# Ranking in two halves, earlier row stores, later x stores, and longer rings for the expert weights

## The chip, the cores and the metric

The program runs on one core of a Trainium2 chip, in fp32. The metric is the device time of one execution in microseconds (us). TensorE (PE), VectorE (DVE), ScalarE (ACT), GpSimd (POOL) and SyncE (SP) each work through their own instruction list in order, and wait for one another by semaphores. SP, ACT and POOL also issue DMA transfers.

## The reference, cut to what matters

There are two layers on 640 tokens: 512 latent ones (`NL`) and 128 context ones (`NC`), of width 1024. Each layer normalizes, modulates (factors computed from the conditioning by `w_mod`), runs two mixers, and then an expert-choice mixture of experts, where each of 16 experts picks its own tokens. This is done for the latent and for the context tokens apart:

```python
def ec_moe(x, w_router, w_gate, w_up, w_down):
    cap = EC_CAPACITY * t // N_EXPERTS          # 64 latent, 16 context
    aff = jax.nn.softmax(logits, axis=1)        # over the tokens
    gate, idx = lax.top_k(aff, cap)
    xs = jax.vmap(lambda xb, ib: xb[ib])(x, idx)
    hid = jax.nn.silu(xs @ w_gate) * (xs @ w_up)      # einsums, 1024 -> 512
    y = (hid @ w_down) * gate[..., None]              # 512 -> 1024
    return jax.vmap(lambda yb, ib: jnp.zeros((t, d), yb.dtype).at[ib].add(yb))(y, idx)
```

## The kernel before

An expert (`e` = 0 to 15) has 80 rows, 64 latent and 16 of the context. Its weights are six pieces of 1 MB (128 partitions x 2048 fp32): `g0`, `g1`, `u0`, `u1` (gate and up) and `d0`, `d1` (down). All weights of the kernel, the expert pieces among them, go through one list, `stream`, which SP works off in order: a piece is loaded into one of four slots of `stage` (`SLOTS`), piece p into slot p modulo 4, after the piece four places ahead of it has been used up. An expert piece m (0 to 95 in a layer, in the order gate and up of e + 1, then down of e) is used up when ACT has written its rounded copy (`w_hi`) and DVE the rest (`w_lo`, semaphore `lo_ready`). PE multiplies three times (hi by hi, hi by lo, lo by hi). Because a load waits on SP, every load behind it waits too.

Before the experts, the start of the MoE (semaphore names in brackets) goes like this:

- DVE ranks the affinities: eight rounds of MAX8, FIND_INDEX8 and MATCH_REPLACE8 over 512 columns, one row for each expert (L2130 to L2138); the context's rows are in the first two rounds. PE turns the lists (`gates`), and DVE writes `slots`, the row numbers.
- PE turns the five row tiles of h (`h`, 128 rows each), ACT evacuates each to one of four row buffers (`htok`) and stores it to `h_dram` (512 KB). The fifth waits until the first store has landed (`h_out`).
- In layer 1, PE also turns the five tiles of x (`x out`), and ACT stores them to `acc_dram` (`x_stored`), to which the experts' results are added.
- ACT writes the context's `slots` (`gates ctx`), behind all those stores in its order.
- POOL gathers the rows of the first four experts from `h_dram` (L780), when `slots` are written and the stores have landed; PE turns them, and the first expert's matmuls start.
- SP's load of piece 4 (L672) waits, besides for its slot, until gather(0) has landed.

For each expert, POOL also scatters: it adds 80 rows to `acc_dram` (L789). A scatter waits for the one before.

The lines of the load of an expert piece, and of the wait for a row buffer:

```python
                        if m == SLOTS:
                            sp.wait_ge(gathered[0], 16 * (E // AHEAD * L + 1))
                        sp.wait_ge(lo_ready, m + (moe_q[L] - SLOTS + 1))
...
                    if t == 4:
                        act.wait_ge(h_out[0], 16 * (2 * L + 1))
```

## Time and profile before

| | us |
|---|---|
| three runs: median (lowest to highest) | 1483.58 (1479.49 to 1487.28) |
| the profiled execution: time | 1485.16 |
| its span, first to last instruction | 1483.4 |
| busy in it: PE | 1275.2 (86%) |
| busy: DVE | 886.8 (60%) |
| busy: ACT | 736.8 (50%) |
| busy: POOL | 218.8 (15%) |

The busy shares are means over the whole execution, and its stages have different limits: each stage is read by itself. A DMA share is the mean busy share of the core's 16 DMA engines. A transfer's time runs from its issue until its data has landed.

### The profile page before, as it was taken

To read this page: it belongs to the slowest core of one execution; us is meant where nothing else is said; L and a number is where in the kernel's file an instruction comes from. 1 tells how busy PE (TensorE), PEld (TensorE's weight loads), DVE (VectorE), ACT (ScalarE), POOL (GpSimd) and SP (SyncE) were. 2 spreads that over 40 slices of the span, in tenths; PEclk is the share of its full clock that TensorE was granted. 3 is DMA by queue.
4 is the path that set the end of the run, shared out by engine and by line. 5 is a ranking of instruction groups with operands and counts; after the bars stand their busy time and mean duration, and the time that the engine had idled before them with its cause. 6 is when DMAs were issued, how large, how long until landed. Compare 5 with 4: busy or idle time off the path is not lost.

```text
span 1483.4 us, 18079 instructions
## 1 busy us (share of the span) xinstructions
PE 1275.2 (86%) x7500; PEld 919.3 (62%) x7500; DVE 886.8 (60%) x997; ACT 736.8 (50%) x866; POOL 218.8 (15%) x128
## 2 busy tenths in 40 slices
PE   5799988997499899999559999999976998999991
PEld 3796856893365555655149994667934655656550
DVE  3613456326688777787164452553257888888883
ACT  3531056415377676776144214453155666666662
POOL 3000000020112121211150000000202023333130
PEclk9897899999699999999779999799997999999996
DMA  9710180004899999999873222002049999999985
GB/s 346 223 61 29 58 298 31 1 29 174 280 324 361 352 355 358 351 366 355 294 211 97 76 61 98 1 1 86 29 170 315 333 351 347 354 347 354 359 311 169
DMA packets 99047, 323.19 MB, mean 218 GB/s; under 512 B 6367, under 2 KB 30142, under 8 KB 82582
## 3 DMA queue, kind: packets, MB, share of 16 engines
q1 hardware_dynamic: 87360, 283.54, 53.3%
q0 software_dynamic: 9152, 30.53, 8.0%
q10 hardware_dynamic: 2454, 7.96, 1.3%
q8 instruction: 60, 0.98, 0.3%
q14 instruction: 21, 0.17, 0.0%
HBM read 298.20 MB, written 23.81 MB: 217 GB/s over the span
## 4 chain that ended last, share of the span: by engine, by line
PE 48%; DMA 21%; ACT 13%; DVE 13%; issue 3%; POOL 1%; ACTq 0%; SPq 0%; POOLq 0%; DVEq 0%
PE psum L821 45%; DVE w_lo L1774 8%; DMA stage<-in_moe_w_up 6%; DMA stage<-in_moe_w_gate 5%; ACT w_hi L1676 5%; DMA stage<-in_moe_w_down 4%; ACT arena L1601 3%; DMA stage<-in_w_mod 2%; DVE arena L2050 2%; DMA h_dram<-arena 1%; DMA acc_dram<-arena 1%; ACT arena L1374 1%; POOL arena L706 1%; DVE h_lo L1774 1%; ACT arena L1423 1%
## 5 line engine op out<-in xcount | busy, mean ns | idle before, releaser
L1774 DVE TENSOR_TENSOR w_lo<-stage,w_hi 128x2048 fp32r<-128x2048 f32 (+1 forms) x216 | 490.7, 2280 | 192.7 <-ACT w_hi L1676 120.7
L1676 ACT ACTIVATE w_hi<-stage 128x2048 fp32r<-128x2048 f32 x192 | 366.6, 1913 | 153.4 <-DMA stage<-in_moe_w_gate 43.0
L821 PE MATMUL psum<-w_hi,h_hi 128*80 128x512 f32 (+1 forms) x848 | 332.4, 392 | 51.8 <-DVE w_lo L1774 40.8
L821 PE MATMUL psum<-w_lo,h_hi 128*80 128x512 f32 (+1 forms) x848 | 326.8, 385 | 0.0
L821 PE MATMUL psum<-w_hi,h_lo 128*80 128x512 f32 (+1 forms) x848 | 326.8, 385 | 0.0
L821 PE MATMUL psum<-h_hi,w_hi 128*128 128x320 f32 x672 | 211.8, 315 | 10.2 <-DVE h_lo L1822 10.2
L821 PEld LDWEIGHTS psum<-w_hi,h_hi 128*80 128x80 f32 (+1 forms) x848 | 130.2, 154 | 132.5 <-DVE w_lo L1774 40.7
L821 PE MATMUL psum<-h_lo,w_hi 128*128 128x320 f32 x672 | 210.3, 313 | 0.0
L821 PE MATMUL psum<-h_hi,w_lo 128*128 128x320 f32 x672 | 210.1, 313 | 0.0
L821 PEld LDWEIGHTS psum<-w_hi,h_lo 128*80 128x80 f32 (+1 forms) x848 | 130.1, 153 | 64.4 <-issue 2.5
L789 POOL DMA_INDIRECT acc_dram<-arena x32 | 94.3, 2946 | 478.7 <-ACT arena L1707 255.0
L821 PEld LDWEIGHTS psum<-w_lo,h_hi 128*80 128x80 f32 (+1 forms) x848 | 130.6, 154 | 53.9 <-issue 2.1
L821 PE MATMUL psum<-arena 128*64 128x128 f32 (+9 forms) x940 | 135.2, 394 | 15.4 <-ACT arena L1601 9.0
L821 PEld LDWEIGHTS psum<-h_hi,w_hi 128*128 128x128 f32 x672 | 128.7, 192 | 12.0 <-issue 12.0
L821 PEld LDWEIGHTS psum<-h_lo,w_hi 128*128 128x128 f32 x672 | 128.7, 191 | 0.2 <-issue 0.2
L821 PEld LDWEIGHTS psum<-h_hi,w_lo 128*128 128x128 f32 x672 | 128.6, 191 | 0.0
L1374 ACT ACTIVATE arena<-psum 128x256 f32<-128x256 f32 (+8 forms) x133 | 75.2, 616 | 103.9 <-PE psum L821 81.6
L821 PEld LDWEIGHTS psum<-arena 128*64 128x64 f32 (+4 forms) x940 | 79.4, 177 | 74.2 <-issue 51.4
L1601 ACT ACTIVATE arena<-psum,arena 128x640 f32<-128x640 f32 x64 | 50.3, 790 | 64.1 <-DVE arena L2050 64.1
L706 POOL TENSOR_TENSOR arena<-arena 128x640 f32<-128x640 f32 x24 | 39.0, 1626 | 282.3 <-ACT arena L1397 280.8
L1387 ACT ACTIVATE w_hi<-stage 128x2048 fp32r<-128x2048 f32 x22 | 42.0, 1913 | 73.6 <-PE psum L821 70.2
L2108 DVE SCALAR_TENSOR_TENSOR xT<-psum,mod,xT 128x320 f32<-128x320 f32 (+2 forms) x48 | 18.2, 434 | 88.1 <-PE psum L821 88.1
(224 smaller groups left out, 1198.5 us busy)
## 6 DMA issues: line engine op xcount, KB each, us to landing
stage<-in_moe_w_gate SPq DMA_DIRECT2D x64, 1024.0 KB, 8.4
stage<-in_moe_w_up SPq DMA_DIRECT2D x64, 1024.0 KB, 8.9
stage<-in_moe_w_down SPq DMA_DIRECT2D x64, 1024.0 KB, 7.3
stage<-in_w_mod SPq DMA_DIRECT2D x48, 1024.0 KB, 7.1
stage<-in_ev_w_in SPq DMA_DIRECT2D x7, 1024.0 KB, 11.8
stage<-in_od_w_in SPq DMA_DIRECT2D x7, 1024.0 KB, 9.9
h_dram<-arena ACTq DMA_DIRECT2D x10, 512.0 KB, 6.7
stage<-in_ev_w_out SPq DMA_DIRECT2D x4, 1024.0 KB, 7.7
```

Of the source, the lines that this page charges most:

```text
L706: nc.gpsimd.tensor_tensor(rstd, rstd, sq[k % 2], ALU.add).then_inc(sq_added, 1)
L789: pool.indirect_dma_start(acc_dram[L], bass.IndirectOffsetOnAxis(slots[:, e:e + 1], 0), ysb[e % 2], None, compute_op=ALU.add).then_inc(sca ...
L821: return pe.matmul(o, w, x, start=first, stop=last, skip_group_check=True)
L1374: freeing(nc.scalar.activation(dst, src, ACT.Copy, **kw))
L1387: nc.scalar.activation(split_slot(w_hi, pc["q"], pc["n"]), slot(pc), ACT.Copy).then_inc(hi_ready, 1)
L1423: ins = nc.scalar.activation(h_sum[k][:, grp], hf[k % 2][:, grp], ACT.Identity, bias=mod[:, L, 3, k, g:g + 1])
L1601: ins = nc.scalar.activation(p[:, LKEYS * a:LKEYS * a + LKEYS], src[:, 0:LKEYS], ACT.Exp, bias=largest(i, a), accum_out=total(i, a))
L1676: nc.scalar.activation(split_slot(w_hi, q0), stage[:, PIECE * (p0 % SLOTS):PIECE * (p0 % SLOTS) + PIECE], ACT.Copy)\
L1774: return nc.vector.tensor_tensor(dst, src, hi.bitcast(F32), ALU.subtract)
L2050: ins = nc.vector.tensor_reduce(largest(i, a), src[:, 0:LKEYS], AX.X, ALU.max, negate=True)
L2108: ins = nc.vector.scalar_tensor_tensor(xT[:, m, tk], src, mod[:, L, 2, m, g:g + 1], xT[:, m, tk], ALU.mult, ALU.add)
```

## The change

**Ranking.** The latent tokens are ranked in two halves of 256 (`NH`): 32 rows, 16 experts by two halves, so each of the eight rounds covers 256 columns. Each half gives a sorted list of 64. A matmul with a mirrored unit matrix (`mirror`, written by POOL) reverses the second list; then the better of high[i] and low[63 - i] is taken, in five small DVE operations, and these are the best 64 of both.

**Row buffers.** `htok` has five buffers, and no evacuation waits for a store. The gather buffers `xs` move to the areas of `h_hi` and `h_lo`. The modulation rows (`ranked`) are computed behind the row tiles and the context's gates.

**x stored behind the gates.** In layer 1, PE turns and ACT stores the tiles of x behind `gates`, `gate rows` and the first two weight splits; PE's first gate matmul waits for the last of these tiles.

**Rings.** The expert pieces go through a ring of places: seven in layer 0, nine in layer 1. Place 4 lies where the sums for h are kept (free when the last row tile is turned and its store has landed), 5 and 6 in the arena (layer 0: free when the last row tile is turned; layer 1: when x is stored), 7 and 8 in `xT` (free when the last tile of x is turned). The wait for gather(0) moves from piece 4 to piece 7 or 9. The pieces of the other weights keep four slots, now counted by `staged_count`; behind layer 0 the count goes on at the slot that the last expert piece used.

```diff
+NH = NL // 2
+TILE_AT = (0, 2, 1, 3, 4)
...
+SUM_PLACES, OUT_PLACES, X_PLACES = (4,), (5, 6), (7, 8)
+PLACES = 9
+LENT_PLACES = {0: SUM_PLACES + OUT_PLACES, 1: SUM_PLACES + X_PLACES + OUT_PLACES}
...
         p.add((L, "aff"), [4], "act"), p.add((L, "aff ctx"), [5], "act")
-        for c in ranked:
-            p.add(("mod rows", c), [6], "act")
         for t in range(NT):
             p.add((L, "h", t), [2 * (t % 3), 2 * (t % 3) + 1], "act")
+        p.add((L, "gates ctx"), [7], "act")
         for c in ranked:
-            p.add(("mod turned", c), [6], "dve", in_order=False)
-        if L == LAYERS - 1:
-            for t in range(NT):
-                p.add(("x out", t), [2 * ((t + 2) % 3), 2 * ((t + 2) % 3) + 1], "act")
-        p.add((L, "gates ctx"), [7], "act")
+            p.add(("mod rows", c), [6], "act"), p.add(("mod turned", c), [6], "dve", in_order=False)
         for c in last:
             p.add(("mod rows", c), [4], "act")
-        p.add((L, "gates"), [5 if L == 0 else 2], "dve")
+        p.add((L, "gates"), [5], "dve"), p.add((L, "mirrored"), [2], "dve")
         for c in last:
             p.add(("mod turned", c), [7], "dve", in_order=False)
         for c in ranked + last:
             p.frees(("mod turned", c))
         if L == LAYERS - 1:
             p.add("gate rows", [7], "act")
+            for t in range(NT):
...
+        s = [(staged_count[0] + i) % SLOTS for i in range(SLOTS)]
+        rings[L] = [*OUT_PLACES, *s, *SUM_PLACES] if L == 0 else [*s, *LENT_PLACES[L]]
         for m in range(6 * E):
             q = sum(x["split"] for x in stream)
-            stream.append(dict(key=(L, "moe", m), split=True, used=("moe_used", 6 * E * L + m + 1), p=len(stream), q=q, n=PIECE))
+            stream.append(dict(key=(L, "moe", m), split=True, used=("moe_used", 6 * E * L + m + 1), p=len(stream), q=q, n=PIECE,
+                               place=rings[L][m % len(rings[L])]))
+        staged_count[0] = s[2] if L == 0 else s[0]
...
+        lent = [place(piece[(1, "lent", n)]["place"]) for n in range(2)]
...
-        htok = [arena[:, at:at + D] for at in (0, 1024, 4096, 5120)]
-        xs = [arena[0:CAP, 2048 + D * s:2048 + D * s + D] for s in range(2)] + \
-            [h_lo_[0:CAP, 1024 + D * s:1024 + D * s + D].bitcast(F32) for s in range(AHEAD - 2)]
+        htok = [arena[:, at:at + D] for at in (0, 1024, 4096, 5120, 2688)]
+        xs = [t[0:CAP, 1024 + D * s:1024 + D * s + D].bitcast(F32) for t in (h_hi_, h_lo_) for s in range(2)]
         ysb = [arena[0:CAP, 4096 + D * s:4096 + D * s + D] for s in range(2)]
-        work, work_both, work_ctx = (arena[rows, 7584:7584 + NL] for rows in (slice(0, E), slice(0, RANKED), slice(CTX_ROW, RANKED)))
+        work, work_both, work_ctx = (arena[rows, 7584:7584 + NH] for rows in (slice(0, 2 * E), slice(0, RANKED), slice(CTX_ROW, RANKED)))
+        mirror, lists = arena[0:CAP_L, 7872:7872 + CAP_L], arena[0:CAP_L, 7936:7936 + 4 * E]
+        first_wins, index_step = arena[0:CAP_L, 8000:8000 + E], arena[0:CAP_L, 8016:8016 + E]
...
                 def expert_piece(e, what):
 
-                    m, m0, half = piece_number(e, what), piece_number(first(e), what), int(what[1])
-                    if isinstance(e, int) and m < SLOTS:
-                        before = stream[moe_p[L] + m - SLOTS]
-                        if before["split"]:
-                            sp.wait_ge(lo_ready, before["q"] + 1)
+                    m, half = piece_number(e, what), int(what[1])
+                    pc, lent_places = stream[moe_p[L] + m], LENT_PLACES[L]
+                    n = pc["place"]
+                    if m < SLOTS + len(lent_places):
+                        if n < SLOTS:
+                            used(sp, pc["earlier"])
+                        elif n in X_PLACES:
+                            filled(sp, ("x out", NT - 1))
                         else:
-                            used(sp, before)
+                            filled(sp, (L, "h", NT - 1))
+                            if n in SUM_PLACES:
+                                sp.wait_ge(h_out[NT - 1], 16 * (L + 1))
+                            elif L == LAYERS - 1:
+                                sp.wait_ge(x_stored, 16 * NT)
                     else:
-                        if m == SLOTS:
+                        if m == SLOTS + len(lent_places):
                             sp.wait_ge(gathered[0], 16 * (E // AHEAD * L + 1))
-                        sp.wait_ge(lo_ready, m + (moe_q[L] - SLOTS + 1))
+                        sp.wait_ge(lo_ready, pc["earlier"]["q"] + 1)
...
+                pool.memset(mirror, 0.0).then_inc(mirror_zeroed, 1)
+                pool.wait_ge(mirror_zeroed, L + 1)
+                pool.affine_select(mirror, mirror, [[1, CAP_L]], ALU.not_equal, 1.0, base=1 - CAP_L, channel_multiplier=1)\
+                    .then_inc(mirror_ready, 1)
                 emptied(pool, (L, "gates ctx"))
-                emptied(pool, (L, "gates"))
-                pool.wait_ge(h_out[0], 16 * 2 * (L + 1))
-                for s in (1, 2, 3):
-                    pool.wait_ge(h_out[s], 16 * (L + 1))
+                emptied(pool, (L, "mirrored"))
+                for t in range(NT):
+                    pool.wait_ge(h_out[t], 16 * (L + 1))
...
-                for t in range(4):
-                    ins = pe.transpose(bank((L, "aff"))[0:E, P * t:P * t + P], aff[:, t, :], ident)
+                for n in range(2):
+                    both_halves = aff[:, 2 * n:2 * n + 2, :].rearrange("p t e -> p (t e)")
+                    ins = pe.transpose(bank((L, "aff"))[0:2 * E, P * n:P * n + P], both_halves, ident)
                 ins.then_inc(psum_full, 1)
                 begin((L, "aff ctx"))
...
-                for c in ranked:
-                    mod_rows(c)
...
-                for c in ranked:
-                    turn_mod(c)
-                if L == LAYERS - 1:
-                    for t in range(NT):
-                        begin(("x out", t))
-                        for k in range(KD):
-                            ins = pe.transpose(pair(("x out", t), n=D)[:, P * k:P * k + P], xT[:, k, P * t:P * t + P], ident)
-                        ins.then_inc(psum_full, 1)
                 pe.wait_ge(ranked_ctx, L + 1)
...
+                for c in ranked:
+                    mod_rows(c)
+                    turn_mod(c)
                 for c in last:
                     mod_rows(c)
                 pe.wait_ge(topk_done, L + 1)
                 begin((L, "gates"))
-                pe.transpose(bank((L, "gates"))[0:CAP_L, 0:E], vals[0:E, :], ident[0:E, 0:E])
-                pe.transpose(bank((L, "gates"))[0:CAP_L, E:2 * E], idxf[0:E, :], ident[0:E, 0:E]).then_inc(psum_full, 1)
+                pe.transpose(bank((L, "gates"))[0:CAP_L, 0:2 * E], vals[0:2 * E, :], ident[0:2 * E, 0:2 * E])
+                pe.transpose(bank((L, "gates"))[0:CAP_L, 2 * E:4 * E], idxf[0:2 * E, :], ident[0:2 * E, 0:2 * E]).then_inc(psum_full, 1)
+                pe.wait_ge(mirror_ready, L + 1)
+                emptied(pe, (L, "gates"))
+                begin((L, "mirrored"))
+                mm(bank((L, "mirrored"))[0:CAP_L, 0:4 * E], mirror, lists, True, True).then_inc(psum_full, 1)
                 for c in last:
                     turn_mod(c)
...
+                    for t in range(NT):
+                        begin(("x out", t))
+                        for k in range(KD):
+                            ins = pe.transpose(pair(("x out", t), n=D)[:, P * k:P * k + P], xT[:, k, P * t:P * t + P], ident)
+                        ins.then_inc(psum_full, 1)
+                emptied(pe, (L, "mirrored"))
...
                 turn_rows(0)
+                if L == LAYERS - 1:
+                    emptied(pe, ("x out", NT - 1))
...
-                evacuate((L, "aff"), work, bank((L, "aff"))[0:E, :])
+                evacuate((L, "aff"), work, bank((L, "aff"))[0:2 * E, 0:NH])
                 evacuate((L, "aff ctx"), work_ctx[:, 0:NC], bank((L, "aff ctx"))[CTX_ROW:RANKED, 0:NC])
-                modulation((L, "rank"))
                 for t in range(NT):
-                    if t == 4:
-                        act.wait_ge(h_out[0], 16 * (2 * L + 1))
-                    evacuate((L, "h", t), htok[t % 4].rearrange("t (k q) -> t k q", k=KD),
+                    evacuate((L, "h", t), htok[t].rearrange("t (k q) -> t k q", k=KD),
                              pair((L, "h", t), n=D).rearrange("t (q k) -> t k q", k=KD))
                     emptied(act, (L, "h", t))
-                    act.dma_start(h_dram[L][P * t:P * t + P, :], htok[t % 4]).then_inc(h_out[t % 4], 16)
-                if L == LAYERS - 1:
-                    for t in range(NT):
-                        evacuate(("x out", t), x_out[t], pair(("x out", t), n=D))
-                        emptied(act, ("x out", t))
...
                 if L == 0:
...
+                modulation((L, "rank"))
+                n0 = E * L
+
...
+                expert_split(0, "g0")
                 modulation((L, "top"))
-                n0 = E * L
...
-                if L == LAYERS - 1:
+                expert_split(0, "g1")
+                if L == 0:
+                    expert_split(0, "u0")
+                else:
                     act.wait_ge(new_out, 16 * 4)
                     evacuate("gate rows", gate_turned, bank("gate rows")[0:2 * KD, 0:P])
                     emptied(act, "gate rows")
                     act.dma_start(gate_dram.rearrange("k g p -> (k g) p"), gate_turned).then_inc(gate_turned_out, 16)
+                    for t in range(NT):
+                        evacuate(("x out", t), x_out[t], pair(("x out", t), n=D))
+                        emptied(act, ("x out", t))
+                        act.dma_start(acc_dram[L][P * t:P * t + P, :], x_out[t]).then_inc(x_stored, 16)
...
                 rows_split(0)
+                if L == LAYERS - 1:
+                    expert_split(0, "u0")
...
-                    rows, from_ = (slice(0, RANKED), work_both) if r < CAP_C // 8 else (slice(0, E), work)
+                    rows, from_ = (slice(0, RANKED), work_both) if r < CAP_C // 8 else (slice(0, 2 * E), work)
...
-                nc.vector.tensor_copy(idxf[0:E, :], idx[0:E, :]).then_inc(topk_done, 1)
+                nc.vector.tensor_copy(idxf[0:2 * E, :], idx[0:2 * E, :]).then_inc(topk_done, 1)
                 filled(dve, (L, "gates"))
+                freeing(nc.vector.tensor_copy(lists, bank((L, "gates"))[0:CAP_L, 0:4 * E]))
+                mirrored = bank((L, "mirrored"))[0:CAP_L, :]
+                high, high_idx, low, low_idx = lists[:, 0:E], lists[:, 2 * E:3 * E], mirrored[:, E:2 * E], mirrored[:, 3 * E:4 * E]
+                filled(dve, (L, "mirrored"))
                 if L == 0:
                     dve.wait_ge(new_out, 32)
-                src = bank((L, "gates"))[0:CAP_L, :]
-                nc.vector.tensor_copy(gates[0:CAP_L, :], src[:, 0:E])
-                freeing(nc.vector.tensor_copy(slots[0:CAP_L, :], src[:, E:2 * E]))
+                nc.vector.tensor_tensor(first_wins, high, low, ALU.is_ge)
+                then(nc.vector.scalar_tensor_tensor(index_step, high_idx, -float(NH), low_idx, ALU.add, ALU.subtract))
+                then(nc.vector.tensor_tensor(index_step, index_step, first_wins, ALU.mult))
+                nc.vector.tensor_tensor(gates[0:CAP_L, :], high, low, ALU.max)
+                freeing(nc.vector.scalar_tensor_tensor(slots[0:CAP_L, :], index_step, float(NH), low_idx, ALU.add, ALU.add))
```

SP's loads at the start of the experts of layer 0, with what each waits for. Before (`arena` and `stage` name where the piece goes; `mod_used` and `psum_full` stand for earlier pieces or tiles that PE has used up, `lo_ready` for a piece that has been split):

```order
L672 DMA stage<-in_moe_w_gate 128x2048 [waits mod_used]
L672 DMA stage<-in_moe_w_gate 128x2048 [waits psum_full]
L672 DMA stage<-in_moe_w_up 128x2048 [waits mod_used]
L672 DMA stage<-in_moe_w_up 128x2048 [waits psum_full]
L672 DMA stage<-in_moe_w_gate 128x2048 [waits lo_ready,gathered0]
L672 DMA stage<-in_moe_w_gate 128x2048 [waits lo_ready]
L672 DMA stage<-in_moe_w_up 128x2048 [waits lo_ready] x2
```

And of the change, at the same place:

```order
L702 DMA arena<-in_moe_w_gate 128x2048 [waits psum_full] x2
L702 DMA stage<-in_moe_w_up 128x2048 [waits mod_used]
L702 DMA stage<-in_moe_w_up 128x2048 [waits psum_full]
L702 DMA stage<-in_moe_w_gate 128x2048 [waits mod_used]
L702 DMA stage<-in_moe_w_gate 128x2048 [waits psum_full]
L702 DMA arena<-in_moe_w_up 128x2048 [waits h_out4,psum_full]
L702 DMA arena<-in_moe_w_up 128x2048 [waits lo_ready,gathered0]
```

The wait for gather(0) has moved from the fifth load to the eighth, and the first two wait for the row tiles. In layer 1 the loads behind the four to `stage` are these (before, they were the same as in layer 0):

```order
L702 DMA arena<-in_moe_w_gate 128x2048 [waits h_out4,psum_full]
L702 DMA xT<-in_moe_w_gate 128x2048 [waits psum_full]
L702 DMA xT<-in_moe_w_up 128x2048 [waits psum_full]
L702 DMA arena<-in_moe_w_up 128x2048 [waits x_stored,psum_full]
L702 DMA arena<-in_moe_w_down 128x2x1024 [waits x_stored,psum_full]
L702 DMA stage<-in_moe_w_down 128x2x1024 [waits lo_ready,gathered0]
```

Five pieces now stand ahead of the wait for gather(0), and two of them wait for the stores of x.

## Rows read from the trace of the kernel before

**Rows 1.** The page's 40 slices: DMA, busy share in tenths.

```profile
DMA  9710180004899999999873222002049999999985
```

**Rows 2.** Windows: us, busy PE, PEld, DVE, ACT, POOL, PE clock, DMA share, GB/s.

```profile
341.00:354.00 13.00, 7.60 (x48) 2.57 (x48) 10.68 (x23) 8.29 (x16) 0.00 (x0) 0.87 1.05 391
...
420.00:460.00 40.00, 39.19 (x189) 25.22 (x188) 33.13 (x20) 30.31 (x23) 8.08 (x4) 1.00 0.97 339
460.00:700.00 240.00, 220.10 (x1037) 139.50 (x1035) 189.25 (x111) 170.23 (x124) 46.76 (x22) 1.00 1.01 356
...
1160.00:1240.00 80.00, 76.75 (x366) 49.30 (x364) 67.56 (x42) 53.72 (x38) 18.71 (x6) 1.00 0.96 336
1240.00:1430.00 190.00, 176.44 (x817) 112.96 (x816) 160.09 (x98) 126.16 (x88) 52.92 (x18) 0.98 1.00 355
```

**Rows 3.** The chain of waits where layer 0's experts start: start, us, what.

```profile
367.33 3.56 PE psum L821 x15
...
373.12 6.71 DMA h_dram<-arena
...
379.86 1.03 ACT arena L1374
...
380.91 8.80 DMA h_dram<-arena
...
390.64 6.16 DMA arena<-h_dram,arena
```

**Rows 4.** Timeline of SP at four places: start, us, operation.

```profile
396.81 0.81 SPq L672 DMA_DIRECT2D stage<-in_moe_w_gate  x2
...
696.33 0.37 SPq L641 DMA_DIRECT2D stage<-in_w_mod  x1
...
709.57 8.97 SPq L641 DMA_DIRECT2D stage<-in_w_mod  x5
...
1137.25 2.35 SPq L672 DMA_DIRECT2D stage<-in_moe_w_gate  x2
```

**Rows 5.** Windows at the start of the experts of both layers.

```profile
388.00:395.00 7.00, 0.00 (x0) 0.00 (x0) 4.74 (x4) 0.00 (x0) 3.96 (x2) 0.50 0.15 39
397.00:420.00 23.00, 19.54 (x82) 12.66 (x83) 13.52 (x8) 10.40 (x8) 1.21 (x2) 0.82 0.98 315
...
1134.00:1140.00 6.00, 1.33 (x8) 1.09 (x8) 4.50 (x2) 4.58 (x4) 5.09 (x4) 0.50 0.74 214
```

**Rows 6.** Timelines of DVE, ACT and POOL where layer 1's experts start.

```profile
1131.00 0.17 DVE L2143 COPY arena<-psum 64x16 f32<-64x16 f32 x1 [0.33 <-PE psum L1271]
1131.10 0.16 DVE L2144 CAST arena<-psum 64x16 uint32<-64x16 f32 x1
...
1132.62 0.16 ACT L1667 ACTIVATE arena<-psum 16x16 uint32<-16x16 f32 x1
...
1133.06 0.98 POOL L780 DMA_INDIRECT arena<-h_dram,arena  x1 [55.72 <-ACT arena L1667]
```

**Rows 7.** Groups of DVE by form, 365 to 390 us: count, busy, mean ns.

```profile
L2130 DVE MAX8 arena<-arena 16x8 f32<-16x512 f32 x6 | 4.1, 682 | 0.2
...
L2133 DVE MATCH_REPLACE8 arena<-arena 16x512 f32<-16x512 f32 x5 | 3.3, 663 | 0.0
```

**Rows 8.** Scatters: the page's group; DMA issues in 1160 to 1240, 1240 to 1430.

```profile
L789 POOL DMA_INDIRECT acc_dram<-arena x32 | 94.3, 2946 | 478.7 <-ACT arena L1707 255.0
...
acc_dram<-arena POOLq DMA_INDIRECT x3, 13.7
...
acc_dram<-arena POOLq DMA_INDIRECT x10, 9.9
```

**Rows 9.** Window behind layer 0's experts.

```profile
709.00:717.00 8.00, 6.20 (x44) 2.63 (x44) 0.54 (x1) 2.99 (x3) 1.40 (x1) 1.00 0.62 160
```

**Rows 10.** DMA queues, 460 to 700 us: packets, MB, share of 16 engines.

```profile
q1 hardware_dynamic: 14105, 77.73, 87.4%
q0 software_dynamic: 2208, 7.54, 13.2%
```

More of the change, by code:

```diff
@@ L296, in piece @@
         q = sum(x["split"] for x in stream)
-        stream.append(dict(key=key, src=src, split=split, used=used, p=len(stream), q=q if split else None, n=n, shape=src.shape[1:]))
+        stream.append(dict(key=key, src=src, split=split, used=used, p=len(stream), q=q if split else None, n=n, shape=src.shape[1:],
+                           place=staged()))
     def rows(w):
@@ L466, in trunk, with place @@
         tmp_o = arena[:, 1280:1280 + NL]
-        lent = [stage[:, PIECE * (piece[(1, "lent", n)]["p"] % SLOTS):][:, 0:PIECE] for n in range(2)]
+        def place(n):
+            if n < SLOTS:
+                return stage[:, PIECE * n:PIECE * n + PIECE]
+            if n in X_PLACES:
+                at = 1024 + PIECE * X_PLACES.index(n)
+                return xT_[:, at:at + PIECE]
+            at = (2048, 9248, 9248 + PIECE)[(SUM_PLACES + OUT_PLACES).index(n)]
+            return arena[:, at:at + PIECE]
+        lent = [place(piece[(1, "lent", n)]["place"]) for n in range(2)]
         qn = v3(arena, 4480, PAIRS, T)
@@ L512, in trunk @@
         freed = {"act": sem("freed_act"), "dve": sem("freed_dve")}
-        stage_in = [sem(f"stage_in{s}") for s in range(SLOTS)]
+        stage_in = [sem(f"stage_in{s}") for s in range(PLACES)]
         hi_ready, lo_ready, mod_used, moe_used = (sem(n) for n in ("hi_ready", "lo_ready", "mod_used", "moe_used"))
@@ L528, in trunk @@
         aff_exp, aff_done, topk_done = (sem(n) for n in ("aff_exp", "aff_done", "topk_done"))
-        h_out = [sem(f"h_out{s}") for s in range(4)]
+        h_out = [sem(f"h_out{s}") for s in range(NT)]
+        mirror_zeroed, mirror_ready = sem("mirror_zeroed"), sem("mirror_ready")
         ranked_ctx, modulated = sem("ranked_ctx"), sem("modulated")
@@ L586, in slot @@
         def slot(pc):
-            s = PIECE * (pc["p"] % SLOTS)
-            return stage[:, s:s + pc["n"]]
+            return place(pc["place"])[:, 0:pc["n"]]
         def arrived(p):
-            return 16 * sum(x["p"] % SLOTS == p % SLOTS and x["key"][1] != "lent" for x in stream[:p + 1])
+            return 16 * sum(x["place"] == stream[p]["place"] and x["key"][1] != "lent" for x in stream[:p + 1])
         def split_slot(t, q, n=PIECE):
@@ L634, in load @@
                     return
-                if pc["p"] >= SLOTS:
-                    before = stream[pc["p"] - SLOTS]
+                before = pc["earlier"]
+                if before is not None:
                     if before["split"]:
@@ L640, in load @@
                         used(sp, before)
-                sp.dma_start(slot(pc).rearrange("p (k n) -> p k n", k=pc["shape"][0]), pc["src"]).then_inc(stage_in[pc["p"] % SLOTS], 16)
+                sp.dma_start(slot(pc).rearrange("p (k n) -> p k n", k=pc["shape"][0]), pc["src"]).then_inc(stage_in[pc["place"]], 16)
             for L in range(LAYERS):
@@ L1278, in _ @@
                     pe.transpose(bank("gate rows")[0:2 * KD, 0:P], mod_blocks_of(L, 5), ident).then_inc(psum_full, 1)
-                if L == LAYERS - 1:
-                    emptied(pe, "gate rows")
-                emptied(pe, (L, "gates"))
+                    for t in range(NT):
[4 more added lines that the diff above has]
+                emptied(pe, (L, "mirrored"))
                 emptied(pe, (L, "h", NT - 1))
@@ L1571, in _ @@
                     for n in range(2):
-                        used(act, stream[piece[(1, "lent", n)]["p"] - SLOTS])
+                        used(act, piece[(1, "lent", n)]["earlier"])
                     for j in range(PAIRS):
@@ L2150, in expert_split @@
                 def expert_split(e, what):
[L2151 to L2154 removed]
+                    pc = stream[moe_p[L] + piece_number(e, what)]
+                    dve.wait_ge(hi_ready, pc["q"] + 1)
+                    rest(split_slot(w_lo, pc["q"]), slot(pc), split_slot(w_hi, pc["q"])).then_inc(lo_ready, 1)
                 def rows_split(e):
```

50 lines of the change are left out of this document (23 added, 27 removed).

## The prediction

> **What bounds the kernel now.** I began with the page's forty slices. The DMA digits are 9 in two long runs, 360 to 690 us and 1110 to 1450 us, and low elsewhere [rows 1]. Those runs are the expert halves (MoE) of the two layers, where SP streams 96 pieces of 1 MB each. The windows there show DMA share 1.01 at 356 GB/s and, in layer 1, 1.00 at 355 GB/s, while PE is busy 220 of 240 us and 176 of 190 us [rows 2]. PE issues 84 matmuls per expert (24 each for gate, up and down, 12 transposes). 1037 matmuls in 240 us make 19.4 us per expert. In 420 to 460 us PE was busy 39.2 of 40 us and did 189, which is 17.8 us per expert [rows 2]. So the steady MoE is bound by the DMA, and PE stands 1.6 us per expert under it. What matters first is therefore DMA time lost before and behind the steady stretch, and only then the DMA's rate.
>
> Then I followed the chain of waits where the first MoE starts. The fifth row tile's evacuation (379.86) waited for the store of the first (373.12 + 6.71); its own store, issued at 380.91, landed 8.80 later; gather(0) started at 390.64 and took 6.16 [rows 3]. SP's load of piece 4, which waits for gather(0), came at 396.81 [rows 4]. Meanwhile the DMA ran at share 0.15 for 7 us, and from 397 to 460 it was below the steady 356 GB/s [rows 5, 2]: four slots had run dry and had to be caught up with.
>
> In layer 1 the last input of gather(0) was not the ranking, whose slots were written at 1131.10 + 0.16, but ACT's copy of the context slots at 1132.62, which stood in ACT's queue behind five x evacuations and their stores; gather(0) went at 1133.06 [rows 6], piece 4 at 1137.25 [rows 4].
>
> **The change part by part.**
>
> *Ranking.* MAX8 and MATCH_REPLACE8 over 512 columns take 0.682 and 0.663 us [rows 7], a 16-column copy 0.17 [rows 6]. I take FIND_INDEX8 as MAX8. The slope is (0.682 - 0.17)/496 = 1.03 ns per column, so 256 columns take about 0.41 us, and the 8 + 8 + 7 operations save 6.0 us (bounds: 0 if the time doesn't follow the columns, 7.8 if it halves). The merge adds a PE transpose, a copy, the mirror matmul and five small DVE operations. At 0.17 each with two hops between engines that is 1.5 to 2 us. Slots are ready some 4.5 us earlier.
>
> *Five row buffers.* The fifth evacuation no longer waits for a landing, and PE's 3.56 us of modulation rows no longer stand before the first transposes [rows 3]. So the first store starts 3 to 4 us earlier, the fifth is issued at about 375 instead of 380.91, and with the same 8.80 it lands at about 384 instead of 389.7 [rows 3]. Both inputs of gather(0) now meet at about 384, 6.6 us earlier. The gather itself now shares the DMA with weights: 6.16 when the queues were idle [rows 3], at worst the 13.7 of a scatter under load [rows 8]; it lands at 390 to 398, against 396.8. So PE starts -1 to 7 us earlier; I take 4, and of it the sum takes nothing by itself, since the DMA holds the end.
>
> *Rings.* In layer 0 the first two pieces now wait for the last row tile's transposes, a few us, while the row stores fill the DMA. Three more pieces than before go out by about 384 (the seventh when the fifth row store has landed), and piece 7 waits for gather(0). Three pieces are 3.15 MB, or 8.8 us at 356 GB/s, and fill the hole of 388 to 395: 7 x 0.85 = -6.0 us of DMA time. The shortfall from 397 to 460 is 23 x (1 - 315/356) + 40 x (1 - 339/356) = 4.6 us [rows 5, 2]; since gather and weights were serial there and are no longer, I take 3.5 of it. **Layer 0: -9.5** (bounds -4, if the gathers come late and PE at its half clock still holds the ring, and -10.6, all of it).
>
> *Layer 1.* With x out behind the gates, the ctx slots are ready when the ranking is, at about 1126; gather(0) goes some 6 us sooner. Piece 4 no longer waits for it: 6 x (1 - 0.74) = 1.6 us [rows 5]. From 1160 to 1240 the DMA had 336 instead of 355 GB/s, 80 x 19/355 = 4.3 us, which a lead of nine pieces should cover. Against that, pieces 7 and 8 wait for x_stored, and pieces 5 and 6 for the x transposes. SP is one queue, so whatever stands behind them waits too. Five x evacuations at 1.03 us [rows 3], each with an issue behind it, take some 7 us, so with a store's landing of 6.7 to 8.8 x_stored comes at about 1142 to 1146, while four stage pieces, pieces 4 to 6 and ten 512 KB stores are 12.6 MB, or 35 us of DMA at 355 GB/s, from about 1113 on. The queue thus stays nearly full; I charge 0.9 us. PE waits for the last x transpose before gate(0), hidden behind gather(0). **Layer 1: -5.0** (bounds +2 and -7).
>
> *End of layer 0.* The next layer's modulation pieces now start at the place of the last expert piece (m = 95) and wait for its split. Before, the first went at 696.33 and four had gone at 709.57 and after [rows 4]. At most that is 13.2 us later, but 709 to 717 had share 0.62, a hole of 3.0 us already [rows 9], and the three pieces that ran ahead had delayed expert pieces, which now land sooner. The hole moves rather than adds: a landing plus both splits is about 5 us against 3.0. **+2** (bounds 0 and +13.2).
>
> *Depth in the steady stretch.* Seven or nine pieces may be outstanding instead of four. Between the bounds 0 (share is 1.01 already) and -35 (430/19.4 = 22 experts of the two steady windows by 1.6 us, down to PE's pace) I stand near zero. The weight queue had 87.4% of the engines' time for 77.73 MB, and the gathers and scatters, 7.54 MB, took 13.2% [rows 10]: together 100.6%, so there are no gaps to fill. But 341 to 354 us reached 391 GB/s with weights only [rows 2], so I leave **-3**. A bound on the other side is the fourth rival. The Trainium skill, "DMA: Bandwidth & Descriptors" (Where 436 GB/s comes from), holds that transfers between HBM and SBUF are bound by HBM at about 358 GB/s; the MoE's 356 agrees, the 391 does not. By that rule depth would give nothing and the sum would be 3 us higher.
>
> *Sum.* -9.5 - 5.0 + 2 - 3 = -15.5 against the profiled execution's 1485.16 us: 1469.7. The median of the runs lies 1.6 us lower, so **1468**. The earlier ranking, gather and stores are inside the layer terms and not added again.
>
> **Rivals.** Within 0.5% (7.4 us) no run of this kernel can be told from no change.
>
> *R2, depth lifts the rate.* If 3% more comes through in the 430 us of steady windows and about 100 us at their edges, 16 us in place of the 3: 1455. Down to PE's pace it would be 35: 1436. For it: the 391 GB/s, and loads that wait for a freed slot. Against it: the 100.6% of engine time. The Trainium skill, "Perfetto Trace Analysis" (Identifying the Most-Contended Engine), calls DMA occupancy misleading and asks for HBM utilization instead; by that rule the full share would not exclude R2.
>
> *R3, the lead is given back.* If the modulation pieces' wait costs all but the old hole, 13.2 - 3.0 = 10.2 instead of 2, and depth gives nothing, the sum is -9.5 - 5.0 + 10.2 = -4.3: 1479, no change that can be told. For it: the modulation chain is on the path between the layers, where nothing else loads the DMA. Against it: the expert pieces land earlier without the three between them.
>
> *R4, slower.* More weight loads outstanding delay the small gathers and scatters. The scatters are serial: each waits for the one before. An issue takes 2.9 us [rows 8] and a landing 9.9 us in 1240 to 1430, so 12.8 of the 19.4 us per expert. It decides from a landing of 16.5 us on. At 18 us the chain is 20.9 us per expert, +1.5 x 32 = +48, less the 12 to 15 gained: about 1517; at 17 us about 1485. Against it: landings took 13.7 us in 1160 to 1240, where the DMA was least loaded, and 9.9 where it was full [rows 8], so load doesn't drive them much.
>
> **How the numbers follow.** Forecast 0.57, R2 0.20, R3 0.17, R4 0.06. The forecast's own range is 1461 to 1475 (its bounds of -4/-10.6, +2/-7 and 0/+13 rarely fall together). The range 1450 to 1480 takes in most of R2 and R3 and leaves out R2's far end and R4. Faster by over 0.5% (below 1476.2): all of R2 and nearly all of the forecast, 0.79; same: R3 less its ends and the forecast's upper edge, 0.15; slower: 0.06.
>
> **What would show it.** Loads of pieces 4 to 6 at 378 to 383 us in layer 0, and no hole in 388 to 395; ranking operations near 0.41 us (a step that fails if they stay above 0.6); gather(0) at about 384 and in layer 1 at about 1127. Steady windows at 353 to 360 GB/s; over 365 speaks for R2. Behind layer 0, the first modulation load right after the last expert piece's split with the DMA empty before it: for 5 us by the forecast, for 10 or more by R3. Scatter landings under 12 us; above 16.5, R4. The prediction is wrong if x_stored comes after about 1150 (the queue of layer 1 runs dry), or if PE, not the DMA, is seen to hold the steady stretch.

## The result and the profile after

The changed kernel takes 1437.57 us (median of 4 runs, 1436.79 to 1438.19) against 1485.18 us: ratio 0.9692, 95% interval 0.9673 to 0.9712. By the medians it is 47.6 us faster; the prediction's sum was 15.5. The profiled execution has a span of 1436.1 us (1483.4 before) and a time of 1438.19.

The page's slices and, of the changed kernel, the windows that answer to [rows 2] and [rows 5] (us, busy PE, PEld, DVE, ACT, POOL, PE clock, DMA share, GB/s):

```profile
DMA  9721073004699999998972312000244999999985
GB/s 335 225 89 32 30 252 118 1 30 176 248 324 354 381 379 380 382 389 320 326 215 88 121 59 89 17 2 16 103 175 174 377 398 379 380 377 386 374 335 167
```

```profile
341.00:354.00 13.00, 7.51 (x50) 2.64 (x49) 9.73 (x21) 6.99 (x13) 0.00 (x0) 0.92 1.05 392
...
388.00:395.00 7.00, 0.00 (x0) 0.00 (x0) 1.06 (x1) 1.91 (x1) 3.73 (x4) 0.50 1.02 413
420.00:460.00 40.00, 40.00 (x193) 25.96 (x192) 33.96 (x21) 31.07 (x23) 8.45 (x4) 1.00 0.93 332
460.00:560.00 100.00, 100.00 (x480) 64.62 (x478) 86.57 (x52) 78.46 (x58) 22.85 (x11) 1.00 1.02 379
...
676.00:687.00 11.00, 8.65 (x40) 5.38 (x39) 6.95 (x5) 5.35 (x5) 1.40 (x1) 1.00 0.23 34
...
1140.00:1200.00 60.00, 60.00 (x288) 38.83 (x287) 53.67 (x34) 43.66 (x31) 14.57 (x5) 1.00 1.02 394
1200.00:1300.00 100.00, 100.00 (x479) 64.63 (x478) 92.58 (x57) 73.00 (x52) 39.10 (x12) 1.00 1.02 377
```

The steady MoE now moves 377 to 394 GB/s at share 1.02, where it moved 356 and 355 at shares 1.01 and 1.00 [rows 2]. PE is busy without a pause in the four long windows: 480 matmuls in 100 us, 17.5 us per expert at 84. The DMA digits look as before, and only the GB/s tell the difference.

Cut at PE's first expert matmul and at the issue of the last scatter of each layer, the two executions differ like this:

| us | before | after | |
|---|---|---|---|
| start to first expert matmul, layer 0 | 399.9 | 401.1 | +1.2 |
| to the last scatter of layer 0 | 314.1 | 290.2 | -23.9 |
| to the first expert matmul of layer 1 | 427.6 | 429.8 | +2.2 |
| to the last scatter of layer 1 | 315.3 | 288.9 | -26.4 |
| to the end | 26.4 | 26.3 | -0.1 |

A second profiled execution of the changed kernel (after_again, below) has 403.2, 291.0, 432.4, 288.5 and 26.7 where the column after stands: two executions of one kernel differ by 2 to 3 us ahead of the experts. All of the gain lies inside the MoEs, and neither starts sooner relative to what stands ahead of it. The chain of waits at the start of layer 0 says why (beside [rows 3]):

```profile
368.60 3.15 PE psum L1282 x16
...
377.12 11.36 DMA h_dram<-arena
388.50 0.04 POOLq L807
...
389.37 8.59 DMA h_hi<-h_dram,arena
397.96 0.14 issue
```

The fifth row store is issued 3.8 us sooner than before but takes 11.36 us in place of 8.80, and the gather takes 8.59 in place of 6.16. Six weight loads go out between 374.8 and 381.4 us, among and behind the stores; before, four did, between 369.3 and 378.6. The runs below show what the loads do to the gather: it takes 5.38 us in ring4 and 4.26 in hold4, where they wait for it. For the store they don't settle it: 9.31 us in ring4, 11.86 in hold4, each with four loads. The gather waited for this store alone, since `slots` were written 5.8 us before it landed (DVE's last operation for them):

```profile
382.56 0.15 DVE L2184 SCALAR_TENSOR_TENSOR arena<-arena,psum 64x16 uint32<-64x16 f32 x1
```

The ranking itself did as expected: the groups of DVE, 368 to 382 us, beside [rows 7]:

```profile
L2164 DVE MAX8 arena<-arena 32x8 f32<-32x256 f32 x6 | 2.5, 416 | 0.2
...
L2167 DVE MATCH_REPLACE8 arena<-arena 32x256 f32<-32x256 f32 x5 | 2.0, 397 | 0.0
```

### The profile page after: what moved, and what is told of

The parts are those of the page before. It is cut to its first block, busy times and chain, and to the rows that moved or that the text cites. A ratio compares the mean times of both kernels' runs of the same rounds, so it can differ in the third digit from the quotient of the medians.

```text
span 1436.1 us, 18100 instructions
## 1 busy us (share of the span) xinstructions
PE 1266.4 (88%) x7500; PEld 917.6 (64%) x7500; DVE 872.5 (61%) x1005; ACT 734.8 (51%) x866; POOL 223.7 (16%) x132
## 4 chain that ended last, share of the span: by engine, by line
PE 72%; DMA 9%; ACT 8%; DVE 7%; issue 2%; POOL 1%; ACTq 0%; SPq 0%; POOLq 0%; DVEq 0%
PE psum L853 69%; ACT arena L1636 3%; DMA stage<-in_w_mod 3%; DVE arena L2084 2%; DMA h_dram<-arena 1%; DMA acc_dram<-arena 1%; DVE w_lo L1808 1%; DMA h_hi<-h_dram,arena 1%; PE psum L1323 1%; DMA arena<-in_moe_w_gate 1%; POOL arena L735 1%; ACT arena L1409 1%; ACT w_hi L1702 1%; DVE h_lo L1808 1%; ACT arena L1458 1%
## 5 line engine op out<-in xcount | busy, mean ns | idle before, releaser
L1808 DVE TENSOR_TENSOR w_lo<-stage,w_hi 128x2048 fp32r<-128x2048 f32 (+1 forms) x123 | 277.6, 2270 | 108.5 <-ACT w_hi L1422 70.5
L1702 ACT ACTIVATE w_hi<-stage 128x2048 fp32r<-128x2048 f32 x99 | 188.4, 1914 | 45.7 <-PE psum L853 40.2
L821 POOL DMA_INDIRECT acc_dram<-arena x32 | 120.9, 3777 | 426.7 <-ACT arena L1739 229.0
L1808 DVE TENSOR_TENSOR w_lo<-arena,w_hi 128x2048 fp32r<-128x2048 f32 x72 | 164.5, 2289 | 31.5 <-ACT w_hi L1702 30.8
L1702 ACT ACTIVATE w_hi<-arena 128x2048 fp32r<-128x2048 f32 x72 | 137.2, 1916 | 28.8 <-PE psum L853 20.4
L853 PE MATMUL psum<-arena 128*64 128x128 f32 (+8 forms) x944 | 135.7, 393 | 16.0 <-ACT arena L1636 9.0
## 6 DMA issues: line engine op xcount, KB each, us to landing
stage<-in_moe_w_gate SPq DMA_DIRECT2D x30, 1024.0 KB, 13.2
```

The costliest lines, as they stand in the source:

```text
L821: pool.indirect_dma_start(acc_dram[L], bass.IndirectOffsetOnAxis(slots[:, e:e + 1], 0), ysb[e % 2], None, compute_op=ALU.add).then_inc(sca ...
L853: return pe.matmul(o, w, x, start=first, stop=last, skip_group_check=True)
L1702: nc.scalar.activation(split_slot(w_hi, pc["q"]), slot(pc), ACT.Copy).then_inc(hi_ready, 1)
L1808: return nc.vector.tensor_tensor(dst, src, hi.bitcast(F32), ALU.subtract)
```

## The experiments

**The theory** after the result: with four slots too few loads are outstanding, and each MB then takes more of the DMA engines' time, which the busy share does not show. **The rivals**: the start edits earn part of it; the addresses of the new places do; PE alone holds the kernel now.

All ratios below are against the kernel before, run beside each on the same chip. Where a text speaks of the experts' time, it is that of the table: from PE's first expert matmul of a layer to the last scatter's issue.

**Rings cut to four slots (ring4).** The rest of the change stays.

```diff
-LENT_PLACES = {0: SUM_PLACES + OUT_PLACES, 1: SUM_PLACES + X_PLACES + OUT_PLACES}
+LENT_PLACES = {0: (), 1: ()}
...
-        rings[L] = [*OUT_PLACES, *s, *SUM_PLACES] if L == 0 else [*s, *LENT_PLACES[L]]
+        rings[L] = [*s, *LENT_PLACES[L]]
...
-        staged_count[0] = s[2] if L == 0 else s[0]
+        staged_count[0] = s[0]
```

> The changed kernel with both rings cut to the four slots of stage; ranking, row buffers and the later x stores stay. Theory (the longer rings keep more loads outstanding, the packets get faster and the DMA's rate rises from 356 to about 380 GB/s; the earlier start is worth nothing): 1478 to 1488 us, as the kernel before, with 353 to 360 GB/s in the steady windows. Rival (the ranking, the buffers and the order of the x stores earn part of the gain): 1455 to 1470 us.

1476.21 us, ratio 0.9963 (0.9935 to 0.9992), 2 us below the theory's range and far above the rival's. Everything but the rings is worth some 5 us here, with the slot order behind layer 0 of before. None of it is in the experts, which take 309.4 and 322.7 us, together 632.1 (before 629.4).

**Rings of five (ring5).**

```diff
+LENT_PLACES = {0: SUM_PLACES, 1: SUM_PLACES}
...
+        rings[L] = [*s, *LENT_PLACES[L]]
...
+        staged_count[0] = s[1]
```

> The changed kernel with rings of five places in both layers (the four slots and place 4). Theory (rate grows with the loads outstanding): between the ends, 1455 to 1470 us, steady windows 362 to 372 GB/s. Rival (only the last places, or the earliest loads ahead of gather(0), matter): 1476 to 1486 us.

1444.55 us, ratio 0.9737 (0.9699 to 0.9775): one place more brings nearly all, more than the theory as it stood expected. The experts take 295.7 and 294.6 us, 590.3 together, where the changed kernel has 579.1; some 5 us of that come back ahead of them (400.0 and 426.0 us). The DMA queues and issues of both, 460 to 660 us (packets, MB, share of 16 engines; then count, KB and median us to landing), first ring4, then ring5:

```profile
q1 hardware_dynamic: 11585, 65.79, 87.9%
q0 software_dynamic: 1949, 6.61, 13.4%
...
stage<-in_moe_w_up SPq DMA_DIRECT2D x21, 1024.0 KB, 9.5
stage<-in_moe_w_down SPq DMA_DIRECT2D x21, 1024.0 KB, 6.8
stage<-in_moe_w_gate SPq DMA_DIRECT2D x20, 1024.0 KB, 9.1
```

```profile
q1 hardware_dynamic: 12365, 69.55, 87.8%
q0 software_dynamic: 2031, 6.94, 14.2%
...
stage<-in_moe_w_up SPq DMA_DIRECT2D x18, 1024.0 KB, 10.9
stage<-in_moe_w_down SPq DMA_DIRECT2D x18, 1024.0 KB, 9.4
stage<-in_moe_w_gate SPq DMA_DIRECT2D x17, 1024.0 KB, 9.2
```

Read three things there. The weight queue's share is the same, but per MB it is 0.879 x 16 x 200/65.79 = 42.8 us of engine time with four slots and 40.4 with five; before it was 0.874 x 16 x 240/77.73 = 43.2 [rows 10]. A piece of 1.049 MB comes every 3.19 us with four and every 3.02 with five. And a landing of about 8.5 us over 3.19 is 2.7 pieces outstanding; of 9.8 over 3.02, 3.2. The other 1.3 to 1.7 slots hold pieces that have landed: 4 x 3.19 - 8.5 = 4.3 us each, which is ACT's 1.91 and DVE's 2.28 us of splitting, one behind the other. That is the missing figure: of four slots, more than one on the mean is in use by the split.

**Seven places in both layers (ring7).**

```diff
+LENT_PLACES = {0: SUM_PLACES + OUT_PLACES, 1: SUM_PLACES + X_PLACES}
```

> The changed kernel with seven places in both layers (layer 1 loses the two that wait for the x stores). Theory: PE is the bound already, so 1436 to 1442 us, layer 1 at 375 GB/s or more. Rival (each place adds its share of the rate): layer 1 gives back two fifths of its 26 us, 1446 to 1450 us.

1441.43 us, ratio 0.9709 (0.9673 to 0.9744). From five places on the rate is level (383, 381 and 382 GB/s in 460 to 660 us with five, seven and the changed kernel); nine places in layer 1 and seven can't be told apart.

**Nine places, but four unsplit pieces (cap4).**

```diff
+                    if m >= SLOTS:
+                        sp.wait_ge(lo_ready, pc["q"] - SLOTS + 1)
                     src = {"g": wg, "u": wu, "d": wd}[what[0]]
```

> The changed kernel with its seven and nine places, but from piece 4 on each load also waits until the piece four ahead of it has been split, so no more than four pieces are unsplit at any time. Theory (the number of loads outstanding sets the rate): 1478 to 1488 us. Rival (where the pieces land, spread over arena, stage and xT, makes the rate): 1437 to 1445 us.

1488.64 us, ratio 1.0041 (1.0017 to 1.0064), with 360 GB/s in 460 to 660 us. That the pieces land in other places doesn't lift the rate; that rival is out. The 12 us over ring4 lie ahead of the experts: these take 309.7 and 316.5 us, but start at 402.1, and 432.8 us behind layer 0's last scatter (ring4: 396.2 and 421.3).

**Four slots, held for less time (halfrest4).** On ring4:

```diff
-rest(split_slot(w_lo, pc["q"]), slot(pc), split_slot(w_hi, pc["q"]))
+rest(split_slot(w_lo, pc["q"], PIECE // 2), slot(pc)[:, 0:PIECE // 2], split_slot(w_hi, pc["q"], PIECE // 2))
```

> The run ring4 (four slots), in which DVE computes the rest of only half of the columns of each expert piece (a change of the result): a slot is held some 1.1 us less after its piece has landed, 3.4 in place of 4.6 us. Theory (four slots less the time that each is held leave too few loads outstanding, 2.6 on the mean): 2.9 outstanding, a piece lands every 3.14 us in place of 3.2 to 3.3, and 192 pieces give 1455 to 1466 us. Rival (five places or more are what the DMA needs, however long they are held): 1470 to 1480 us.

1443.18 us, ratio 0.9722 (0.9683 to 0.9761), 33 us under ring4 (run on another chip) and 12 below the expected range. DMA queue and issues, 460 to 660 us:

```profile
q1 hardware_dynamic: 12270, 68.86, 88.1%
...
stage<-in_moe_w_up SPq DMA_DIRECT2D x22, 1024.0 KB, 10.0
stage<-in_moe_w_down SPq DMA_DIRECT2D x22, 1024.0 KB, 7.5
stage<-in_moe_w_gate SPq DMA_DIRECT2D x22, 1024.0 KB, 9.2
```

That is a piece every 3.05 us, 8.9/3.05 = 2.9 outstanding, 4 x 3.05 - 8.9 = 3.3 us held (ACT's 1.91 and DVE's 1.23), and 40.9 us of engine time per MB. So four slots do most of it if each is given back a microsecond sooner, and it is the loads outstanding that count rather than the number of places. It is not all: the experts take 295.7 and 303.9 us, 599.6 together, so 2.9 outstanding bring 33 of the 53 us between ring4's 632.1 and the changed kernel's 579.1, and ring5's 3.2 bring 42. The rest of the time comes from ahead of the experts (397.3 and 423.3 us). One rival stands: DVE also does half the splitting here (99.8 us busy in 460 to 660, against 159.9), and this run can't tell a lighter DVE from the earlier release. ring5, with DVE at 170.8, shows that a lighter DVE isn't needed.

**Rings alone (rings_only).** The kernel before with the rings and the moved gather buffers; ranking, row buffers and orders of before.

```diff
+rings[L] = [*OUT_PLACES, *s, *SUM_PLACES] if L == 0 else [*s, *LENT_PLACES[L]]
...
+xs = [t[0:CAP, 1024 + D * s:1024 + D * s + D].bitcast(F32) for t in (h_hi_, h_lo_) for s in range(2)]
```

> The kernel before with nothing but the rings of seven and nine places (and the gather buffers moved out of their way): one ranking over 512, four row buffers, the old order of row tiles, x stores and modulation rows. Theory (the rings carry nearly all of it): 1442 to 1452 us. Rival (the rings need the earlier start and the later x stores to be of use): 1455 to 1470 us.

1444.41 us, ratio 0.9756 (0.972 to 0.9793); the experts take 290.6 and 287.9 us. Beside it, on the same chip, **the changed kernel again (after_again)**:

> The changed kernel itself, beside the others on the same chip: 1434 to 1441 us by every theory.

1442.14 us, ratio 0.9717 (0.9683 to 0.9751). It runs above the expectation: three of its four runs took 1442 to 1444. The intervals overlap: with the rings in, the other parts are worth 2 us, too little to tell from nothing.

**One ranking over 512 (rank512).** The changed kernel without halves, mirror and merge.

```diff
-                    rows, from_ = (slice(0, RANKED), work_both) if r < CAP_C // 8 else (slice(0, 2 * E), work)
+                    rows, from_ = (slice(0, RANKED), work_both) if r < CAP_C // 8 else (slice(0, E), work)
...
-                mm(bank((L, "mirrored"))[0:CAP_L, 0:4 * E], mirror, lists, True, True).then_inc(psum_full, 1)
```

> The changed kernel with one ranking over 512 columns again, without mirror and merge. Theory (the row stores are the last input of gather(0), so the faster ranking is worth nothing): 1436 to 1440 us. Rival (the ranking is on the path in both layers, some 5 us each): 1445 to 1449 us.

1446.36 us, ratio 0.9763 (0.9741 to 0.9785), the rival's time but not its reason. (The interval lies above the changed kernel's 0.9673 to 0.9712 and touches after_again's.) In its trace gather(0) of layer 0 starts at 390.79, as in after_again (390.82): there the ranking is off the path. What costs is layer 1, where the x stores stand behind the ranking and two places wait for the stores. SP's timeline there, rank512 and then the changed kernel:

```profile
1120.61 1.00 SPq L702 DMA_DIRECT2D xT<-in_moe_w_up  x1
1139.05 0.33 SPq L702 DMA_DIRECT2D arena<-in_moe_w_up  x1
```

```profile
1111.79 0.61 SPq L702 DMA_DIRECT2D xT<-in_moe_w_up  x1
1129.90 0.33 SPq L702 DMA_DIRECT2D arena<-in_moe_w_up  x1
```

SP stands still for 17 us in both, and until 14.0 us past PE's first expert matmul (1125.0) in the one, 8.9 us (1121.0) in the other. From that matmul to the last scatter it is 293.0 us against 288.9 (after_again 288.5). So once x is stored behind the gates, the ranking is on a path again; rings_only, which ranks over 512 but stores x early, doesn't pay this.

**Two passes of three (twopass9).** Every expert product leaves out its third matmul.

```diff
+            def passes2(o, w, x, first, last):
+                mm(o, w[0], x[0], first, False)
+                return mm(o, w[0], x[1], False, last)
...
-                        ins = passes(psum[0:CAP, b, :], (x_hi[:, kk, :], x_lo[:, kk, :]), (hi[:, k, :], lo[:, k, :]),
+                        ins = passes2(psum[0:CAP, b, :], (x_hi[:, kk, :], x_lo[:, kk, :]), (hi[:, k, :], lo[:, k, :]),
```

> The changed kernel, which leaves out the third of the three matmul passes of every expert product (a change of the result). PE then needs some 12.5 us per expert in place of 17.6. Theory (the DMA's own ceiling with deep rings lies just above what PE takes): the steady windows at 385 to 400 GB/s, 1425 to 1437 us. Rival (PE alone held the changed kernel and the DMA has much room left): over 410 GB/s, 1400 to 1420 us.

1431.39 us, ratio 0.9652 (0.9622 to 0.9683). Its windows:

```profile
460.00:660.00 200.00, 153.98 (x668) 91.49 (x668) 171.38 (x102) 153.11 (x111) 44.80 (x20) 0.95 1.02 384
1200.00:1380.00 180.00, 137.21 (x604) 81.89 (x603) 162.45 (x101) 128.35 (x91) 146.22 (x19) 0.94 1.02 382
```

With PE idle a quarter of the time the DMA moves 384 and 382 GB/s, no more than in the changed kernel. Nor do places hold it: in layer 0 a landing of 16 to 17.5 us over a piece every 3.01 us is more than five of seven loading. So as far as these runs show the DMA's own ceiling for this mix is there, at 18.0 us per expert, close to PE's 17.5: the two are level. Taking work from PE alone brings 10 us in layer 0 (280.5 in place of 290.2) and nothing in layer 1 (290.3).

**Where the room is left.** Three variants of the changed kernel at its starts and at the end of layer 0.

The first, mods3:

```diff
-        staged_count[0] = s[2] if L == 0 else s[0]
+        staged_count[0] = s[3] if L == 0 else s[0]
```

> The changed kernel; behind layer 0 the modulation pieces start at the slot whose last expert piece is m = 89 instead of m = 95, so the four slots come free one after the other. Theory (the wait for the last expert piece opens a hole of some 8 us in the DMA, and the modulation that waits for those pieces is on the path to layer 1): 4 to 8 us less, 1429 to 1434 us. Rival (the hole is hidden behind the reload of x): 1435 to 1440 us.

1434.67 us, ratio 0.9693 (0.967 to 0.9716). From the last scatter of layer 0 to the first expert matmul of layer 1 it takes 423.6 us in place of 429.8, but layer 1's experts take 1.5 more; by the times, just above the theory's range and below the rival's, it can't be told from the changed kernel.

The second, hold4:

```diff
+                    if m == SLOTS:
+                        sp.wait_ge(gathered[0], 16 * (E // AHEAD * L + 1))
```

> The changed kernel with the wait for gather(0) back at piece 4 in both layers; the rings stay at seven and nine. Theory (the added loads at the start delay the row stores and the gather, and PE, now the bound, starts later for it): gather(0) lands 3 to 5 us sooner in each layer and the time falls by 4 to 9 us, 1429 to 1434 us. Rival (the pieces ahead are what the rate lives on, and the hole in the DMA comes back): 1441 to 1447 us.

1438.58 us, ratio 0.9722 (0.9693 to 0.9751), between the two ranges. The profiled execution was its fastest (1432.44). Its chain at the start of layer 0 has the gather thus:

```profile
374.25 11.86 DMA h_dram<-arena
...
387.00 4.26 DMA h_hi<-h_dram,arena
...
394.34 10.59 PE psum L855 x36
```

PE starts 6.7 us sooner and keeps 5.9 of it to the last scatter of layer 0. Not all of this is the edit's: the ranking, which stands ahead of it, already starts 3.2 us sooner (365.9 against 369.1). In layer 1 what the start gains (3.8 us from the last scatter to the first expert matmul) the experts lose (292.8 against 288.9).

The third, hold0_mods3, is mods3 with the wait of hold4 in layer 0 alone:

```diff
+                    if m == SLOTS and L == 0:
```

> The changed kernel with the slot order of mods3 behind layer 0, and with piece 4 waiting for gather(0) in layer 0 alone. Theory (the start of layer 0 gains some 6 us from the earlier gather, the transition some 5, and layer 1 keeps its pieces ahead): 1425 to 1430 us. Rival (the DMA hole that it opens in layer 0 is paid for in its steady stretch, where DMA and PE are level): 1433 to 1440 us.

1434.08 us, ratio 0.9674 (0.9646 to 0.9701), 4 us over the theory's range and in the rival's. Layer 0's experts take 291.0 us from a start at 397.3, so the rival's reason isn't seen; what the theory missed is behind it, where the transition takes 426.5 us and layer 1's experts 292.1. Beside the changed kernel on the same chip (after_again) it is 8 us faster (1431.18 to 1435.55 against 1435.05 to 1443.75), but the intervals of the ratios overlap. Of the versions that compute the whole result it has the lowest ratio, and it can't be told from mods3 or the changed kernel.

## Why the prediction was wrong

**The bound.** That the steady MoE was held by the DMA and PE stood 1.6 us per expert under it was right; PE now goes at 17.5 us per expert, near that pace. The sign that the prediction set against itself, PE holding the steady stretch, came (100.00 of 100.00 us busy). PE holds it on its lead: a piece every 3.04 us is 18.2 us per expert, so it uses up pieces faster than they land.

**Depth in the steady stretch: the step that failed.** It put 87.4% and 13.2% of engine time together to "no gaps to fill" and left -3. There were no gaps, but the busy time was not a fixed amount of work: with 2.7 loads outstanding an MB took some 43 us of engine time, with 3.2 or more 40.4. The weight queue in 460 to 660 us, before and then after:

```profile
q1 hardware_dynamic: 11325, 63.81, 86.9%
```

```profile
q1 hardware_dynamic: 12296, 69.01, 87.1%
```

That is a piece every 3.29 and every 3.04 us, and 96 times the difference is 24 us, an estimate (a few pieces land before the first matmul), against the 23.9 of layer 0. In layer 1 it is 3.26 and 3.01 (57.86 and 62.68 MB in 1200 to 1380 us), 24 of the 26.4. So the term was some -48, not -3. The bound of -35 was too small as well, as it counted only the 22 experts inside two windows. R2 named this mechanism, at 0.20; the result came at its far end (1436), which the range left out. R2's sentence on the Trainium skill, "Perfetto Trace Analysis" (Identifying the Most-Contended Engine), that DMA occupancy misleads and HBM utilization is to be read, agrees with these runs: share 1.02 at 363 and at 383 GB/s. The limit of some 358 GB/s that the Trainium skill, "DMA: Bandwidth & Descriptors" (Where 436 GB/s comes from), gives for HBM, a core's half of what a stack gives to two, did not bind here: the MoE runs at 377 to 394.

**Layer 0, -9.5, and layer 1, -5.** The hole of 388 to 395 is filled (share 1.02), as said, and 1140 to 1200 stands at 394 GB/s. But the shorter period accounts for nearly all of -23.9 and -26.4, so hardly anything is left that the filled holes could have brought. hold4 and hold0_mods3, which hold those loads back again in layer 0, agree: in hold4 the DMA share is 0.84 in 381 to 389 us and 0.93 in 389 to 398, yet the layer's experts take 291.0 us in both runs, as in after_again. Nor does an earlier start always bring what it seems to: in ring4 PE starts 3.7 us earlier in layer 0 and keeps it, and 6.3 us earlier behind its last scatter in layer 1, but there the experts take 322.7 in place of 315.3 us.

**Gather at 384 and 1127.** Wrong: 389.37 in layer 0. The fifth store went out at 377.12, not at about 375, and its landing of 8.80 was carried over to another mix of stores and loads (11.36). In layer 1, 1108.49, which is 18.6 us behind the ranking's start in place of 20.4: 1.8 us sooner, not 6, as the fifth row store was the last input there too (issued at 1098.32, landed 9.32 us later). The first expert matmul comes 12.5 us behind it where it had been 8.6. Where a change puts other transfers beside one, its duration doesn't carry over.

**Ranking.** 0.416 us against 0.41 forecast. It is off the path in layer 0, where the forecast had both inputs of gather(0) meet, but on one in layer 1 (rank512).

**End of layer 0, +2.** From there to layer 1 it is +2.2, and +4.8 in after_again; but that stretch holds the start of layer 1 as well, so the agreement is luck in part. The first modulation load goes behind the last split (686.82), and four go out together:

```profile
686.82 2.17 SPq L666 DMA_DIRECT2D stage<-in_w_mod  x4
```

The DMA before it runs at share 0.23 for 11 us (676 to 687), 8.5 us empty where the forecast had 5 and R3 10 or more. mods3, which lets these loads go sooner, takes 6.2 us off that stretch.

**R3 and R4.** R3's time didn't come, though its hole nearly did; R4 didn't. Scatters land in 9.9 us at the median in 460 to 660 and 12.9 in 1140 to 1380, with nearly twice the loads ahead; R4 needed 16.5.

## What to carry to other kernels

A DMA share of 1.0 doesn't say that the DMA is at its ceiling: divide the engines' busy time by the MB moved, and compare with a stretch that has more loads outstanding. Count slots by their cycle: those held by the work behind the landing (here 4.3 us of a 12.8 us cycle) load nothing, so a place more, or a sooner release, can be worth more than any edit at the edges. An earlier start of PE can be paid back inside the experts, as it was in layer 1 of ring4 and of hold4, and it can be kept, as in layer 0 of both: it has to be followed to the end of the stretch. And two profiled executions of one kernel differ by 2 to 3 us in a stretch, so a variant worth less needs more than one trace.

## What the runs showed of the hardware

The weight queue's engine time per MB falls as more 1 MB loads are outstanding, at an unchanged busy share. In 460 to 660 us it is 42.8 us at 2.7 outstanding (ring4; 43.6 before, 43.1 in cap4), 40.9 at 2.9 (halfrest4), 40.4 at 3.2 (ring5) and no less at 4.6 (the changed kernel, landing 13.9 us at the median). Layer 1 says the same in 1200 to 1380 us: 44.3, 42.0, 40.5 and 40.3 for ring4, halfrest4, ring5 and the changed kernel. As the share hardly moves, this is the rate told in another way, and it names no cause.

The packets show where the time is. Over the 8 KB packets of 460 to 660 us the median is 314 to 318 ns in all these runs, but the slowest tenth takes at least 460 ns before, 452 in ring4, 456 in cap4, 428 in halfrest4, 407 in ring5 and 333 in the changed kernel (374 in after_again). What an engine does in these slow packets no view here shows; that stays open.
